# Head outputs of two attention branches with tokens on partitions: squares summed along the free axis, the mLSTM denominator as one more column, transposes back

## Chip, cores and metric

One core of a Trainium2 chip runs the whole program. The metric is the device time of one execution in microseconds (us); lower is better.

## The reference, cut to what matters

Two transformer blocks run over 256 tokens of width 1024, all in fp32. The change touches the middle of the first block, where a differential attention (8 heads of width 128) and an mLSTM (4 heads of width 256) run side by side, each head's output is RMS-normalised, and both go through a projection.

```
def diff_attention(q, k, v, lam, g_subln, lambda_init):
    ...
        a = p[:, 0] - lam * p[:, 1]
        return jnp.einsum('bhqk,bkhd->bqhd', a.astype(v.dtype), v)
    ...
    o = rmsnorm(o, g_subln) * (1.0 - lambda_init)
...
        sc = jnp.einsum('bhtd,bhsd->bhts', qc, kc) * w
        ...
        den = jnp.sum(sc, axis=-1) + w_inter * jnp.einsum('bhtd,bhd->bht', qc, n)
        h = num / jnp.maximum(jnp.abs(den), jnp.exp(-m_t))[..., None]
...
    hn = rmsnorm(hcell, g_mlnorm.reshape(H, Dh))
    y = (hn + ml_skip.reshape(H, Dh) * xch) * jax.nn.sigmoid(o_pre).reshape(B, S, H, Dh)
...
        merged = jax.nn.sigmoid(ga) * (ya @ w_proj_a[l]) + jax.nn.sigmoid(gb) * (yb @ w_proj_b[l])
```

## The kernel before

Activations lie transposed: features on the 128 partitions, the 256 tokens (T) along the free axis. A linear layer is `t_linear`: one call computes 256 output features by 16 matmuls of 128x128 weights against 256 tokens. In the trace each fp32 matmul is two records, so one call is 32 records; a transpose is one record. Weights stream through four slots of 2 MB (`W`, `slots`), fetched by SyncE in a fixed order, each as soon as its slot's last reader is done.

The order of every engine is written out by hand, one Python loop over iterations j for each engine; engines meet only at semaphores. The stretch of the change is the mixer loop of the first block, j = 0 to 31. On TensorE an iteration holds some small work of the heads and then one linear call (iterations 16 to 27: `ga`, `gb`, `op`; 28 to 31: `pa`), and after the loop come four `pb` calls. Small work around the change, by iteration:

- 12 to 19: attention scores of head j-12 (`t_da_scores`), whose softmax takes VectorE (`v_da_scores`), ScalarE (`s_da_exp`) and VectorE (`v_da_weights`) in turn. 14 to 21: transpose of the weights (`t_da_turn`, head j-14). 15 to 22: the product with the values (`t_da_mix`, head j-15), copied by ScalarE into YA (`s_da_mix`).
- 18 to 25: even, mLSTM scores (`t_ml_scores`, which also spreads two rows over all partitions as "ml b"); odd, `t_ml_mix`: the numerator, and with a block of ones the denominator, spread over all partitions.
- 24 and 26: `t_squares`, 8 matmuls that sum ScalarE's squares over the partitions, for attention ("dn") and mLSTM ("hn"). 25 to 31: `t_spread`, 12 matmuls that lay the resulting 1/rms rows over all partitions, which VectorE multiplies in (`v_da_norm`, `v_ml_out`).

PSUM banks go round in rings: `L` (banks 0 to 2: linear calls and the transposes of `t_ada_turn`), `S3` (banks 3 to 5: attention scores, two a head, attention products, mLSTM scores and numerators), `X2` (banks 6 and 7: the rest). `open` gives the next bank of a ring and waits until the user three (S3) or two (X2) places earlier has closed it. `ABT` holds attention and mLSTM weights; two of its four buffers go round as `ab`. VectorE also sums the modulation vectors from weights in the slots (`v_ada_blocks`, rows tmpA<-slots), which frees these slots.

## Time and profile before

| what | value |
|---|---|
| three runs, median (lowest, highest) | 1405.17 us (1404.03, 1406.8) |
| the profiled execution, its own time | 1407.13 us |
| its span, first to last instruction | 1405.0 us |
| TensorE busy | 1368.4 us, 97% of the span |
| VectorE, ScalarE, GpSimd busy | 586.3, 286.5, 40.6 us |
| mean granted TensorE clock | 0.995 |

The profile is of one execution; times in it are from the start of its span. L197 is the helper behind all matmuls, L200 transposes, L203 ScalarE's activations, L206, L209, L212 and L215 forms of VectorE work. A record's duration includes the pipeline's depth, and neighbours overlap, so the cost of a piece of TensorE work is read from its start to the start of the next piece. PE is TensorE, PEld its weight loads, DVE VectorE, ACT ScalarE.

### The profile page before, as it was taken

How to read it: one execution, taken by the hardware profiler on the slowest of the kernel's cores; microseconds unless marked ns; L12 is line 12 of the kernel's file. 1: busy time of each engine (PE TensorE's matmuls, PEld its weight loads, DVE VectorE, ACT ScalarE, POOL GpSimd, SP SyncE). 2: the span in 40 equal slices, each digit the busy share in tenths (PEclk: the TensorE clock that was granted, in tenths of full speed). 3: DMA queues.
4: the chain of work that ended last, by engine and by line, in shares of the span. 5: the costliest groups of instructions: out<-in, count | busy, mean ns of one | idle time of the engine just before them, and what ended most of it. 6: DMA issues, size and time to landing. Idle time of an engine off the chain costs nothing.

```text
span 1405.0 us, 17698 instructions
## 1 busy us (share of the span) xinstructions
PE 1368.4 (97%) x7428; PEld 1164.3 (83%) x7428; DVE 586.3 (42%) x1513; ACT 286.5 (20%) x770; POOL 40.6 (3%) x46
## 2 busy tenths in 40 slices
PE   4999999999999999999999999999999999899997
PEld 3888888976778877889888889988799999577777
DVE  4536440150165444544464620377643231056642
ACT  2100000221143221003000001332323321044431
POOL 0000000000110000010000000000200000000010
PEclk8999999999999999999999999999999999999999
DMA  9788854633535335585898754453300513632300
GB/s 327 231 300 288 299 176 155 229 101 114 186 110 190 108 132 180 198 298 194 298 299 288 267 181 147 156 204 121 104 17 1 180 61 120 185 91 61 121 1 30
DMA packets 170092, 236.99 MB, mean 169 GB/s; under 512 B 4924, under 2 KB 106350, under 8 KB 170014
## 3 DMA queue, kind: packets, MB, share of 16 engines
q1 hardware_dynamic: 166736, 229.40, 48.8%
q10 hardware_dynamic: 2542, 3.31, 0.7%
q0 software_dynamic: 736, 3.17, 0.6%
q8 instruction: 58, 0.95, 0.3%
q14 instruction: 20, 0.16, 0.0%
HBM read 234.79 MB, written 4.22 MB: 170 GB/s over the span
## 4 chain that ended last, share of the span: by engine, by line
PE 94%; DVE 3%; ACT 1%; DMA 1%; issue 0%; POOL 0%; SPq 0%; DVEq 0%; ACTq 0%
PE ps L197 91%; PE ps L200 4%; DMA slots<-in_w_down 1%; DMA H<-in_xT 1%; DVE tmpB L212 0%; ACT tmpC L203 0%; DVE U L212 0%; DVE tmpA L212 0%; DVE rstd L224 0%; DVE arena L212 0%; DVE mods L221 0%; ACT arena L203 0%; ACT U L203 0%; DVE arena L206 0%; POOL arena L206 0%
## 5 line engine op out<-in xcount | busy, mean ns | idle before, releaser
L197 PE MATMUL ps<-U,slots 128*128 128x256 f32 (+2 forms) x3488 | 720.1, 366 | 3.0 <-ACT U L203 2.4
L197 PEld LDWEIGHTS ps<-U,slots 128*128 128x128 f32 (+1 forms) x3488 | 618.4, 190 | 86.6 <-issue 7.5
L197 PE MATMUL ps<-arena,slots 128*128 128x256 f32 (+1 forms) x1840 | 325.8, 338 | 3.4 <-DMA slots<-in_w_down 2.6
L197 PEld LDWEIGHTS ps<-arena,slots 128*128 128x128 f32 x1840 | 292.2, 191 | 34.9 <-DMA slots<-in_w_down 3.0
L212 DVE SCALAR_TENSOR_TENSOR tmpA<-slots,sm,tmpA 128x512 f32<-128x512 f32 x182 | 139.3, 765 | 5.9
L203 ACT ACTIVATE tmpC<-ps 128x256 f32<-128x256 f32 (+3 forms) x97 | 39.8, 414 | 438.0 <-PE ps L197 426.3
L197 PE MATMUL ps<-arena 128*128 128x64 f32 (+6 forms) x736 | 110.3, 308 | 1.5 <-ACT arena L203 0.9
L197 PEld LDWEIGHTS ps<-arena 128*128 128x128 f32 (+1 forms) x736 | 90.7, 190 | 21.9 <-issue 16.1
L203 ACT ACTIVATE arena<-ps 128x512 f32<-128x512 f32 (+1 forms) x90 | 48.2, 547 | 178.2 <-PE ps L197 137.6
L212 DVE SCALAR_TENSOR_TENSOR tmpC<-tmpC,ps 128x256 f32<-128x256 f32 (+2 forms) x48 | 19.6, 407 | 140.1 <-ACT tmpC L203 140.0
L212 DVE SCALAR_TENSOR_TENSOR H<-ps,sm,H 128x256 f32<-128x256 f32 (+1 forms) x32 | 11.9, 413 | 135.4 <-PE ps L197 135.4
L203 ACT ACTIVATE tmpC<-H 128x512 f32<-128x512 f32 (+1 forms) x32 | 16.3, 520 | 240.0 <-DVE H L212 217.7
L203 ACT ACTIVATE arena<-arena,st 128x128 f32<-128x128 f32 (+2 forms) x128 | 48.4, 404 | 20.6 <-DVE st L209 20.6
L197 PE MATMUL ps<-tmpC,cst 128*128 128x128 f32 (+1 forms) x256 | 37.6, 304 | 10.9 <-ACT tmpC L203 10.8
L212 DVE SCALAR_TENSOR_TENSOR tmpB<-arena,hw,tmpB 128x256 f32<-128x256 f32 x96 | 46.5, 485 | 3.4
L197 PEld LDWEIGHTS ps<-tmpC,cst 128*128 128x128 f32 (+1 forms) x256 | 31.7, 194 | 15.1 <-issue 9.6
L212 DVE SCALAR_TENSOR_TENSOR arena<-tmpC,ps 128x512 f32<-128x512 f32 x16 | 11.0, 686 | 72.9 <-ACT tmpC L203 72.9
L203 ACT ACTIVATE U<-U,mods,sm 128x128 f32<-128x128 f32 (+1 forms) x72 | 29.9, 493 | 54.2 <-DVE sm L212 42.8
L200 PE MATMUL ps<-cst,arena 128*128 128x128 f32 (+1 forms) x288 | 39.8, 276 | 0.0
L200 PEld LDWEIGHTS ps<-cst,arena 128*128 128x128 f32 (+1 forms) x288 | 31.5, 140 | 7.5 <-issue 3.2
L227 DVE COPY arena<-ps 64x256 f32<-64x256 f32 (+4 forms) x18 | 7.8, 432 | 63.3 <-PE ps L197 63.1
L203 ACT ACT_TABLE_LOAD x24 | 30.8, 1283 | 3.9 <-issue 1.8
(142 smaller groups left out, 807.0 us busy)
## 6 DMA issues: line engine op xcount, KB each, us to landing
slots<-in_w_ada SPq DMA_DIRECT2D x14, 2048.0 KB, 7.9
slots<-in_w_in SPq DMA_DIRECT2D x14, 2048.0 KB, 8.0
slots<-in_ada_w SPq DMA_DIRECT2D x12, 2048.0 KB, 8.1
slots<-in_w_down SPq DMA_DIRECT2D x16, 1408.0 KB, 6.9
slots<-in_w_gate SPq DMA_DIRECT2D x19, 1024.0 KB, 5.6
slots<-in_w_up SPq DMA_DIRECT2D x19, 1024.0 KB, 8.6
slots<-in_a_in_w SPq DMA_DIRECT2D x8, 2048.0 KB, 8.9
slots<-in_b_in_w SPq DMA_DIRECT2D x12, 1024.0 KB, 5.6
```

Source lines behind the costliest of these rows:

```text
L197: return Nothing() if self.e is None else self.e.matmul(*a, **k)
L200: return Nothing() if self.e is None else self.e.transpose(*a, **k)
L203: return Nothing() if self.e is None else self.e.activation(*a, **k)
L212: return Nothing() if self.e is None else self.e.scalar_tensor_tensor(out=o, in0=i0, scalar=s, in1=i1, op0=op0, op1=op1)
L227: return Nothing() if self.e is None else self.e.tensor_copy(*a)
```

## The change

Both products are computed the other way round: the attention weights or mLSTM scores are the stationary operand and the values move, so that an output has tokens on partitions and a head's features along the free axis.

- `t_da_mix` is three matmuls of 128 columns instead of one of 256 and one of 128. ScalarE sums squares along the free axis as it reads the bank (`accum_out`), and VectorE and ScalarE make the 1/rms of all 16 (head, token half) columns in three small steps. VectorE scales YA (`v_da_scale`, iterations 24 and 25), TensorE transposes it back (`t_da_flip`, 26 and 27, two calls of four transposes each), and ScalarE copies with the gain (`s_da_norm`).
- `t_ml_mix` is three matmuls of 257 columns: MV has a column of ones behind each head, so that column 256 is the denominator. It takes two banks of S3, one for each token half, and waits for both at its start. The matmuls with a block of ones are gone. ScalarE reads each bank four times (`s_ml_mix`). The division is folded into the normalisation, and `v_hn_scale` (26 and 27), `t_hn_flip` (28 to 31, four transposes each) and `v_ml_out` follow.
- "ml b" spreads one row instead of two; the floor row becomes a column by two more small transposes in `t_ml_source` (iteration 13), which now also wait for ScalarE's exponential of that row.
- `t_squares`, `t_spread` and their partners are gone, and the constant `selc` with them (64 columns). The skip term is scaled by ScalarE beforehand (`s_skip`, one in each iteration from 18 to 25). One memset writes the ones.

Not shown in the diff: `v_da_mean`, `s_da_root`, `v_da_rstd`, `v_hn_mean`, `s_hn_root` and `v_hn_rstd` work on at most 16 columns; `v_hn_scale` and `t_hn_flip` are to mLSTM what `v_da_scale` and `t_da_flip` are to attention, one call a head. Lines of which only the removal matters are left to the listing above.

```diff
-        def t_squares(e, n, row_of, to=X):
...
-            for h in range(8):
-                e.wait_ge(*act.at(n, "sq", h // 2))
-                e.matmul(ps[0:8, 0:T], selc[:, row_of(h), :], TC.buf(n, "sq", h // 2)[:, h % 2 * T:h % 2 * T + T], start=h == 0,
-                         stop=h == 7).then_inc(*pe.up(n, "sq", h))
-        def t_spread(e, n, h, row, to=X):
...
-            e.matmul(ps[:, 0:T], row_to_all(h, 8), row).then_inc(*pe.up(n, "row", h))
...
         def t_da_mix(e, h):
...
-            aT = at_.buf("da", h)
-            e.matmul(ps[:, 0:T], VA[:, 0, h * P:(h + 1) * P], aT[:, 0:T], start=True, stop=False)
-            e.matmul(ps[:, 128:T], VA[:, 1, h * P:(h + 1) * P], aT[:, 256:384], start=False, stop=True).then_inc(*pe.up("da mix", h))
+            aT, v0, v1 = at_.buf("da", h), VA[:, 0, h * P:(h + 1) * P], VA[:, 1, h * P:(h + 1) * P]
+            e.matmul(ps[:, 0:P], aT[:, 0:P], v0)
+            e.matmul(ps[:, P:T], aT[:, P:T], v0, start=True, stop=False)
+            e.matmul(ps[:, P:T], aT[:, T:384], v1, start=False, stop=True).then_inc(*pe.up("da mix", h))
             at_.close([pe.now()], "da", h)
         def s_da_mix(e, h):
+            ps = S3.buf("da mix", h)
             e.wait_ge(*pe.at("da mix", h))
-            e.activation(YA[:, h, :], S3.buf("da mix", h)[:, 0:T], ACT.Copy).then_inc(*act.up("ya", h))
+            e.activation(YA[:, h, :], ps[:, 0:T], ACT.Copy).then_inc(*act.up("ya", h))
+            for i in range(2):
...
+                e.activation(jk, ps[:, i * P:(i + 1) * P], ACT.Square, accum_out=ss[:, 2 * h + i:2 * h + i + 1]).then_inc(*act.up())
+                JK.close([act.now()], "da", h, i)
+            act.mark("ya sq", h)
             S3.close([act.now()], "da mix", h)
...
+        def v_da_scale(e, g):
+            y = YA[:, 2 * g:2 * g + 2, :].rearrange("p h (i n) -> p (h i) n", i=2)
+            e.wait_ge(*dve.at("dn rstd"))
+            e.wait_ge(*act.at("ya", 2 * g + 1))
+            e.tensor_tensor(y, y, ss[:, 4 * g:4 * g + 4].unsqueeze(2).to_broadcast([P, 4, P]), ALU.mult).then_inc(*dve.up("dn", g))
+        def t_da_flip(e, g):
...
+            e.wait_ge(*dve.at("dn", g))
+            for n in range(4):
+                i = e.transpose(ps[:, n * P:(n + 1) * P], YA[:, 2 * g + n // 2, n % 2 * P:n % 2 * P + P], ident)
+            i.then_inc(*pe.up("da flip", g))
+        def s_da_norm(e, g):
+            e.wait_ge(*pe.at("da flip", g))
+            e.activation(YA[:, 2 * g:2 * g + 2, :], two(X2.buf("da flip", g)), ACT.Copy, scale=V("g_subln")).then_inc(*act.up("ya out", g))
+            X2.close([act.now()], "da flip", g)
...
-        MV = arena[:, 14368:16416].rearrange("p (i n) -> p i n", i=2)
+        MV = arena[:, 14368:16424].rearrange("p (i h n) -> p i h n", i=2, h=4)
...
-            e.matmul(ps, row_to_all(h, 4), R[0:4, 4:6, :]).then_inc(*pe.up("ml b", h))
+            e.matmul(ps[:, 0:T], row_to_all(h, 4), R[0:4, 4, :]).then_inc(*pe.up("ml b", h))
...
         def t_ml_mix(e, h):
             sc = ab.buf("ml", h)
-            np_, free = S3.open("ml n", h)
-            for f in free:
+            n0, free = S3.open("ml n", h, 0)
+            n1, free2 = S3.open("ml n", h, 1)
+            for f in free + free2:
                 e.wait_ge(*f)
             e.wait_ge(*dve.at("ml sc", h))
-            for e2 in range(2):
-                o = h * T + e2 * P
-                e.matmul(np_[:, e2 * T:(e2 + 1) * T], MV[:, 0, o:o + P], sc[:, 0:T], start=True, stop=False)
-                i = e.matmul(np_[:, e2 * T + P:(e2 + 1) * T], MV[:, 1, o:o + P], sc[:, T:384], start=False, stop=True)
-            i.then_inc(*pe.up("ml n", h))
-            dp, free = X2.open("ml den", h)
-            for f in free:
-                e.wait_ge(*f)
-            e.matmul(dp[:, 0:T], C("ones"), sc[:, 0:T], start=True, stop=False)
-            e.matmul(dp[:, P:T], C("ones"), sc[:, T:384], start=False, stop=True).then_inc(*pe.up("ml den", h))
+            e.wait_ge(*dve.at("ml ones"))
+            e.matmul(n0[:, 0:257], sc[:, 0:P], MV[:, 0, h, :])
+            e.matmul(n1[:, 0:257], sc[:, P:T], MV[:, 0, h, :], start=True, stop=False)
+            e.matmul(n1[:, 0:257], sc[:, T:384], MV[:, 1, h, :], start=False, stop=True).then_inc(*pe.up("ml n", h))
             ab.close([pe.now()], "ml", h)
...
+        HT = HC.rearrange("p (h i) n -> p h i n", i=2)
+        den, hsq = gates[:, :, 24:28], gates[:, :, 20:24]
+        hs2 = gates[:, :, 28:36].rearrange("p i (n h) -> p i n h", n=2)
+        def s_ml_mix(e, h):
             e.wait_ge(*pe.at("ml n", h))
+            for i in range(2):
+                ps = S3.buf("ml n", h, i)
+                e.activation(HT[:, h, i, :], ps[:, 0:T], ACT.Copy).then_inc(*act.up("ht", h, i))
+                e.activation(den[:, i, h:h + 1], ps[:, T:257], ACT.Abs).then_inc(*act.up())
+                for n in range(2):
...
+                    e.activation(jk, ps[:, n * P:(n + 1) * P], ACT.Square, accum_out=hs2[:, i, n, h:h + 1]).then_inc(*act.up())
+                    JK.close([act.now()], "ml", h, i, n)
+                S3.close([act.now()], "ml n", h, i)
+            act.mark("ht sq", h)
...
+        def s_skip(e, c):
+            e.wait_ge(*pe.at("mk", 3))
+            e.activation(XC[:, c, :], XC[:, c, :], ACT.Copy, scale=sm[:, 120 + c:121 + c]).then_inc(*act.up("skip", c))
...
                     t_ml_source(e)
                 if 18 <= j < 26:
                     (t_ml_mix if j % 2 else t_ml_scores)(e, (j - 18) // 2)
-                if j == 24:
-                    t_squares(e, "dn", lambda h: h, X2)
-                if 25 <= j < 29:
-                    t_spread(e, "dn", 2 * j - 50, r8, X2)
-                    t_spread(e, "dn", 2 * j - 49, r8, X2)
-                if j == 26:
-                    t_squares(e, "hn", lambda c: c // 2, X2)
+                if 26 <= j < 28:
+                    t_da_flip(e, 2 * j - 52)
+                    t_da_flip(e, 2 * j - 51)
                 if 28 <= j < 32:
-                    t_spread(e, "hn", j - 28, r8h, X2)
+                    t_hn_flip(e, j - 28)
                 if j >= 18 and j % 4 == 2:
                     t_ada_turn(e, 12 + (j - 18) // 4)
                 if j < 4:
...
                 elif j < 28:
                     t_linear(e, ("ga", "gb", "op")[(j - 16) // 4], j % 4, U, u_in("n2"))
                 else:
-                    t_linear(e, "pa", j - 28, YA, lambda k, half: dve.at("ya", k))
+                    t_linear(e, "pa", j - 28, YA, lambda k, half: act.at("ya out", k // 2))
...
                     v_da_scores(e, j - 12)
                 if 10 <= j < 18:
                     v_rotate(e, ("q", "k")[j % 2], (j - 10) // 2)
-                if 18 <= j < 26:
-                    (v_ml_mix if j % 2 else v_ml_scores)(e, (j - 18) // 2)
+                if 18 <= j < 26 and j % 2 == 0:
+                    v_ml_scores(e, (j - 18) // 2)
                 if j == 24:
-                    v_mean(e, "dn", 1.0 / 128, 0.8, r8, X2)
-                    v_rstd(e, "dn", r8)
-                if 25 <= j < 29:
-                    v_da_norm(e, 2 * j - 50)
-                    v_da_norm(e, 2 * j - 49)
+                    v_da_mean(e)
+                    v_da_rstd(e)
+                if 24 <= j < 26:
+                    v_da_scale(e, 2 * j - 48)
+                    v_da_scale(e, 2 * j - 47)
                 if j == 26:
-                    v_mean(e, "hn", 1.0 / 256, 1.0, r8h, X2)
-                    v_rstd(e, "hn", r8h)
+                    v_hn_mean(e)
+                    v_hn_rstd(e)
+                if 26 <= j < 28:
+                    v_hn_scale(e, 2 * j - 52)
+                    v_hn_scale(e, 2 * j - 51)
                 if 28 <= j < 32:
                     v_ml_out(e, j - 28)
                 if j >= 29:
...
                 if j == 13:
                     s_ml_floor(e)
                 if 18 <= j < 26:
-                    (s_ml_den if j % 2 else s_ml_weights)(e, (j - 18) // 2)
+                    (s_ml_mix if j % 2 else s_ml_weights)(e, (j - 18) // 2)
+                    s_skip(e, j - 18)
                 if 12 <= j < 20:
                     s_da_exp(e, j - 12)
-                if j == 23:
-                    s_squares(e, "dn", YA, lambda h: act.at("ya", h))
                 if j == 24:
-                    s_rstd(e, "dn", r8)
-                if j == 25:
-                    s_squares(e, "hn", HC, lambda c: dve.at("hc", c))
+                    s_da_root(e)
                 if j == 26:
-                    s_rstd(e, "hn", r8h)
+                    s_hn_root(e)
+                if 26 <= j < 28:
+                    s_da_norm(e, 2 * j - 52)
+                    s_da_norm(e, 2 * j - 51)
```

In iteration 19 TensorE has, before, the transposes of attention head 5 (into ps6), the scores of head 7 (ps5 and ps3, q and k from arena), and the numerator (ps4) and denominator (ps7) of mLSTM head 0; the buffer numbers are the banks:

```order
L200 MATMUL ps6<-cst,ABT 128x128 x3
L197 MATMUL ps5<-arena 128x128
L197 MATMUL ps5<-arena 128x256
L197 MATMUL ps3<-arena 128x128
L197 MATMUL ps3<-arena 128x256
L197 MATMUL ps4<-ABT,arena 128x256
L197 MATMUL ps4<-ABT,arena 128x128
L197 MATMUL ps4<-ABT,arena 128x256
L197 MATMUL ps4<-ABT,arena 128x128
L197 MATMUL ps7<-ABT,cst 128x256
L197 MATMUL ps7<-ABT,cst 128x128
L197 MATMUL ps1<-U,slots 128x256 x16
```

and with the change:

```order
L196 MATMUL ps6<-cst,ABT 128x128 x3
L193 MATMUL ps5<-arena 128x128
L193 MATMUL ps5<-arena 128x256
L193 MATMUL ps3<-arena 128x128
L193 MATMUL ps3<-arena 128x256
L193 MATMUL ps4<-arena,ABT 128x257
L193 MATMUL ps5<-arena,ABT 128x257 x2
L193 MATMUL ps1<-U,slots 128x256 x16
```

Six matmuls, all with 256 or 128 columns, have become three of 257 columns, and their second bank is ps5, which the first scores of head 7 were written to just ahead.

In iterations 26 to 29 TensorE has, before, spreads (ps<-rows,cst), the sums of mLSTM squares (ps<-tmpC,cst), a modulation transpose (ps<-cst,tmpA) and the linear calls:

```order
L197 MATMUL ps<-rows,cst 128x256 x2
L197 MATMUL ps<-tmpC,cst 8x256 x8
L200 MATMUL ps<-cst,tmpA 128x128 x4
L197 MATMUL ps<-U,slots 128x256 x16
L197 MATMUL ps<-rows,cst 128x256 x2
L197 MATMUL ps<-U,slots 128x256 x16
L197 MATMUL ps<-rows,cst 128x256 x3
L197 MATMUL ps<-arena,slots 128x256 x16
L197 MATMUL ps<-rows,cst 128x256
L197 MATMUL ps<-arena,slots 128x256 x16
```

and with the change:

```order
L196 MATMUL ps<-cst,arena 128x128 x8
L196 MATMUL ps<-cst,tmpA 128x128 x4
L193 MATMUL ps<-U,slots 128x256 x16
L196 MATMUL ps<-cst,arena 128x128 x8
L193 MATMUL ps<-U,slots 128x256 x16
L196 MATMUL ps<-cst,arena 128x128 x4
L193 MATMUL ps<-arena,slots 128x256 x16
L196 MATMUL ps<-cst,arena 128x128 x4
L193 MATMUL ps<-arena,slots 128x256 x16
```

Each spread, and the sums of squares, have made way for transposes of YA and HC (ps<-cst,arena); the linear calls stand as they did.

## Rows read from the trace of the kernel before

**Rows 1.** The page: busy times (first section), and shares of the chain that ended last.

```profile
PE 1368.4 (97%) x7428; PEld 1164.3 (83%) x7428; DVE 586.3 (42%) x1513; ACT 286.5 (20%) x770; POOL 40.6 (3%) x46
...
PE 94%; DVE 3%; ACT 1%; DMA 1%; issue 0%; POOL 0%; SPq 0%; DVEq 0%; ACTq 0%
```

**Rows 2.** Windows: stretch, length, busy of PE, PEld, DVE, ACT, POOL, clock, DMA.

```profile
445.00:583.50 138.50, 138.22 (x656) 111.24 (x656) 64.54 (x136) 31.05 (x68) 0.00 (x0) 1.00 0.46 164
```

**Rows 3.** Timeline of PE, iterations 18 and 19: start, length, operation, records.

```profile
446.55 1.12 PE L197 MATMUL ps<-rows,cst 4*128 4x512 f32 x2
447.60 1.57 PE L197 MATMUL ps<-arena 128*128 128x256 f32 x8
...
456.36 0.82 PE L197 MATMUL ps<-ABT,arena 128*128 128x256 f32 x4
457.01 0.49 PE L200 MATMUL ps<-cst,ABT 128*128 128x128 f32 x3
...
458.30 1.57 PE L197 MATMUL ps<-ABT,arena 128*128 128x256 f32 x8
...
460.36 7.07 PE L197 MATMUL ps<-U,slots 128*128 128x256 f32 x32
```

**Rows 4.** Timeline of PE, iterations 24 and 25.

```profile
509.64 3.62 PE L197 MATMUL ps<-tmpC,cst 128*8 128x256 f32 x16
513.20 7.17 PE L197 MATMUL ps<-U,slots 128*128 128x256 f32 x32
...
522.26 1.24 PE L197 MATMUL ps<-rows,cst 8*128 8x256 f32 x4
523.43 7.17 PE L197 MATMUL ps<-U,slots 128*128 128x256 f32 x32
```

**Rows 5.** Timeline of PE, iterations 28 to 31 and three calls behind them.

```profile
552.90 7.17 PE L197 MATMUL ps<-arena,slots 128*128 128x256 f32 x32
560.00 0.69 PE L197 MATMUL ps<-rows,cst 8*128 8x256 f32 x2
560.62 7.17 PE L197 MATMUL ps<-arena,slots 128*128 128x256 f32 x32
...
576.47 27.89 PE L197 MATMUL ps<-arena,slots 128*128 128x256 f32 x128
```

**Rows 6.** Timeline of PE, eight full transposes in iteration 9.

```profile
353.23 1.04 PE L200 MATMUL ps<-cst,arena 128*128 128x128 f32 x8
354.10 7.15 PE L197 MATMUL ps<-U,slots 128*128 128x256 f32 x32
```

**Rows 7.** Groups of PE by form: records, busy us, mean ns of one.

```profile
L197 PE MATMUL ps<-arena,slots 128*128 128x128 f32 x736 | 84.5, 275 | 0.0
```

**Rows 8.** Timeline of VectorE, iteration 19: weights of head 6, then scores of head 7.

```profile
457.61 0.29 DVE L209 TENSOR_SCALAR ABT<-arena,st 128x128 f32<-128x128 f32 x1 [4.96 <-PE ps L200]
...
459.20 0.42 DVE L215 CUSTOM_DVE_ANT_0 arena<-ps,cst 128x256 f32<-128x256 f32 x1
...
459.54 0.29 DVE L215 CUSTOM_DVE_ANT_0 arena<-ps,cst 128x128 f32<-128x128 f32 x1
```

**Rows 9.** Timeline of ScalarE, iteration 19: exponentials with accumulated sums.

```profile
460.84 0.39 ACT L203 ACTIVATE arena<-arena,st 128x128 f32<-128x128 f32 x1
...
461.23 0.50 ACT L203 ACTIVATE arena<-arena,st 128x256 f32<-128x256 f32 x1
```

**Rows 10.** Groups of ScalarE by form, 399 to 585 us.

```profile
L203 ACT ACTIVATE arena<-ps 128x256 f32<-128x256 f32 x8 | 3.1, 383 | 0.3
```

**Rows 11.** DMA: issue in SyncE's timeline.

```profile
565.71 0.37 SPq L233 DMA_DIRECT2D slots<-in_w_proj_b  x1
```

**Rows 12.** DMA issues of the page: KB each, us from issue to landing.

```profile
slots<-in_w_proj_b SPq DMA_DIRECT2D x2, 2048.0 KB, 9.7
```

**Rows 13.** Windows, columns as in rows 2: behind an idle stretch, and among transposes.

```profile
20.00:28.00 8.00, 1.48 (x5) 1.11 (x6) 7.04 (x12) 1.09 (x2) 0.00 (x0) 0.65 1.10 348
1027.00:1049.00 22.00, 21.75 (x200) 21.64 (x200) 10.63 (x25) 4.18 (x7) 0.00 (x0) 1.00 0.01 1
```

More of the change, by code:

```diff
@@ L325, in build @@
         one_row = rows[0:8, 7, :]
-        r8, r8h = rows[0:8, 0, :], rows[0:8, 3, :]
         def parts(key):
@@ L1040, in build @@
         TILES = [(0, 0, 128, 128), (1, 128, 384, 0)]
+        JK = ring(*[arena[:, 21416 + P * n:21544 + P * n] for n in range(3)])
+        ss = sm[:, 140:156]
         def t_da_scores(e, h):
@@ new lines, in t_da_flip @@
+        def t_da_flip(e, g):
+            ps, free = X2.open("da flip", g)
+            for f in free:
+                e.wait_ge(*f)
+            e.wait_ge(*dve.at("dn", g))
[6 more added lines that the diff above has]
+            X2.close([act.now()], "da flip", g)
@@ L1339, in s_ml_weights @@
         def s_ml_weights(e, h):
[L1340 to L1343 removed]
+            w_ = TB.buf("ml", h)
             e.wait_ge(*dve.at("ml d", h))
[L1345 removed]
             e.wait_ge(*dve.at("ml source"))
@@ L1371, in t_ml_mix, with v_hn_rstd, v_hn_scale, t_hn_flip @@
+        def v_hn_rstd(e):
+            e.wait_ge(*act.at("hn root"))
+            e.reciprocal(hsq, hsq).then_inc(*dve.up("hn rstd"))
+        def v_hn_scale(e, h):
+            e.wait_ge(*dve.at("hn rstd"))
+            e.tensor_tensor(HT[:, h, :, :], HT[:, h, :, :], hsq[:, :, h:h + 1].to_broadcast([P, 2, T]), ALU.mult).then_inc(*dve.up("hn", h))
+        def t_hn_flip(e, h):
+            ps, free = X2.open("hn flip", h)
             for f in free:
                 e.wait_ge(*f)
-            e.wait_ge(*dve.at("ml sc", h))
@@ L1404, in v_ml_out @@
-        def v_ml_out(e, h):
-            ps = X2.buf("hn", "row", h)
-            e.wait_ge(*pe.at("hn", "row", h))
+            e.wait_ge(*dve.at("hn", h))
+            for n in range(4):
+                j = e.transpose(ps[:, n * P:(n + 1) * P], HT[:, h, n % 2, n // 2 * P:n // 2 * P + P], ident)
+            j.then_inc(*pe.up("hn flip", h))
+        def s_skip(e, c):
+            e.wait_ge(*pe.at("mk", 3))
+            e.activation(XC[:, c, :], XC[:, c, :], ACT.Copy, scale=sm[:, 120 + c:121 + c]).then_inc(*act.up("skip", c))
@@ L2489, in vector @@
             e.memset(XM[:, :, 0:3], 0.0).then_inc(*dve.up("xm pads"))
+            e.memset(MV[:, :, :, T:257], 1.0).then_inc(*dve.up("ml ones"))
             e.wait_ge(*dve.at("xm pads"))
```

124 lines of the change are left out of this document (50 added, 74 removed).

## The prediction

> **What bounds the kernel now.** I read the page first. TensorE is busy for 97% of the span and has 94% of the chain that ended last; the other engines are at 42% or less [rows 1]. A change is therefore worth what it does to TensorE's own list of work, plus any wait that it puts into that list. The windows view says the same of the stretch that is changed: from 445.0 to 583.5 us TensorE is busy for 138.22 of 138.50 us at a clock of 1.00, VectorE for 64.5 and ScalarE for 31.1 us [rows 2]. So there is almost no wait to win here. I then priced each piece by the timeline of TensorE, from its start to the next piece's start, since the printed durations overlap.
>
> **What TensorE loses.**
> - "ml b" with two rows (512 columns) takes 1.05 us, 446.55 to 447.60 [rows 3]. One row of 256 columns over all partitions is what a single spread is, 0.62 us, 560.00 to 560.62 [rows 5]. Four times 0.43: −1.7 us.
> - Numerator and denominator of an mLSTM head take 2.06 us, 458.30 to 460.36 [rows 3], of 1152 columns in all. In their place stand three matmuls of 257 columns. No row has that width; four calls in a row give 27.89 us for 64 matmuls of 256 columns, 0.436 us each [rows 5], so three take about 1.31 us (one column more is under 1%). The edges to neighbouring work cost some 0.05 us that stay: 0.70 us less, four times, −2.8 us. The lower end is nothing more than this, the upper end for an odd width that streams badly is the price of the old piece: 0 instead of −2.8.
> - The sums of squares go: 8 matmuls in 3.56 us, 509.64 to 513.20 [rows 4], twice: −7.1 us.
> - The spreads go: two in 1.17 us, 522.26 to 523.43 [rows 4], one alone in 0.62 [rows 5]; twelve at 0.60 are −7.2 us.
> - A linear call in front of a spread takes 7.10 us, 552.90 to 560.00, against 6.97 (27.89 / 4) without one [rows 5]. Six such edges: −0.8 us.
>
> **What TensorE gains.**
> - 32 full transposes of YA and HC and two tiny ones. Eight transposes take 0.87 us, 353.23 to 354.10 [rows 6], 0.109 us each: 34 × 0.109 = +3.7 us. Their upper bound is the price of an ordinary matmul of 128 columns, 0.23 us (below), which would be +7.8; I take 0.109 because the row is of the same operation from the same memory.
> - The attention product becomes three matmuls of 128 columns. Before it takes 0.65 us, 456.36 to 457.01 [rows 3]. Of 128-column records 736 take 84.5 us, 0.115 each, two a matmul [rows 7]: 0.23 us, so three are 0.69. The changed operand roles cost no extra loads that show: +0.04, eight times, +0.3 us.
>
> **Waits that the change adds.** A numerator now takes two banks of S3 where it took one, and waits for both at its start. In iteration 19 its second bank (ps5) holds the first scores of attention head 7, which TensorE wrote just ahead. VectorE frees that bank only after the weights of head 6, which themselves wait for the transposes of head 5 on TensorE. Before, VectorE starts these weights at 457.61, begins the last reduction of the first scores at 459.20 and goes over to the second bank at 459.54 [rows 8]; with its accumulator read the bank is free at about 459.6, and a semaphore later, 459.7, TensorE may go on. TensorE was at the numerator at 458.30 [rows 3]. Both sides hang on the same transposes, so the distance stays: **+1.4 us**, once. Behind the waiting matmul stand linear call 19 and all later work. In iterations 21, 23 and 25 there are no new attention scores, and the places three earlier in the ring are banks that ScalarE emptied, or VectorE read for the scores that the numerator needs in any case; I cost them at nothing.
>
> ScalarE gets more to do. An accumulating activation of 128 columns takes 0.39 us to the next start, 460.84 to 461.23 [rows 9], a copy of 256 columns 0.38 [rows 10]. `s_da_mix` grows by 0.8 us, `s_ml_mix` is at most 8 × 0.39 = 3.1 us, `s_skip` 0.4. The fullest iteration, 19, has 18 activations, about 18 × 0.4 = 7 us, against more than 8 on TensorE (a linear call of 7.0 and a numerator of 1.3 alone); readers need its results an iteration later. In iterations 20 to 25 the exponentials are gone. VectorE gets less to do. For nothing I also take the memset, the additional wait in `t_ml_source` (the exponential behind it is short and ScalarE has the time), and the smaller constant; if any shows, it is a few tenths.
>
> The transposes back wait for long chains, but with an iteration of about 7 us between each link and its reader: squares of head 7 in iteration 22, roots and scaling in 24 and 25, `t_da_flip` from 26; numerator of head 3 in 25, root and scaling in 26 and 27, `t_hn_flip` from 28. Its bank in X2 was emptied by ScalarE an iteration before. That is the cover; a link that took more than 7 us would lose it, and each microsecond over would be lost once.
>
> **Weights.** A faster TensorE asks for weights sooner. The first `pb` block is issued at 565.71 [rows 11] and lands 9.7 us later [rows 12], at 575.4; its call starts one linear call behind 576.47, at 583.4 [rows 5]. That leaves 8 us. The issue hangs on VectorE's sum in iteration 29, which follows TensorE, so issue and reader move together; work of only about 1 us is removed between them. Behind the stretch nothing is changed, and each fetch is released by a reader, so the gain should be carried to the end.
>
> **Sum.** −1.7 − 2.8 − 7.1 − 7.2 − 0.8 + 3.7 + 0.3 + 1.4 = −14.2 us. The profiled execution took 1407.13 us, so one like it would take 1392.9. The median of the three runs is 2.0 us lower, 1405.17; from it I get **1391.0 us**.
>
> **Rivals.**
> 1. *The wait in iteration 19 is not alone.* The ring of three banks is short for a numerator of two. If ScalarE's four reads a bank are slower from PSUM than the rows say, mLSTM scores and attention products in iterations 20 to 24 wait for banks too. At 1.4 us, as in iteration 19, for each of three more iterations it would be −14.2 + 4.2, about 1395.2 us. Or the odd width costs its 2.8 us, about 1393.8. For it: such waits come from ScalarE's order, which is fixed. Against it: ScalarE is busy for only 31.1 of 138.5 us [rows 2].
> 2. *No wait at all.* If something ahead on TensorE takes the 1.4 us, 1389.6 us. Rows 8 speak against it.
> 3. *The gain is given back to the weights.* If transfers, and not readers, set the pace behind 583 us, up to all 14.2 us are lost: 1403 to 1405 us, no change. Against it are the 8 us above.
> 4. *Slower: the clock falls.* At 20 to 28 us TensorE has idle stretches and its granted clock is 0.65 [rows 13]. If the wait in iteration 19 and then groups of up to 12 transposes did the same, the 60 us of work from 523.43 [rows 4] to 583.4 would run at 1.2 instead of 2.4 GHz: +60 − 14.2, about 1451 us. It decides for slower as soon as more than 14 us of work run at the lower level. Against it: from 1027 to 1049 us TensorE alternates transposes with short matmuls, and the clock is 1.00 [rows 13]. The Trainium skill has this rule ("TensorE: Matmul & The Clock Gate", Part 4: PE-mode transpose): transposes don't count as busy TensorE for the clock gate. By that rule the change puts 32 of them where full matmuls stood; the trace has not borne it out where other matmuls stand between them.
> 5. *The change is not what it says,* as where another instruction holds what was removed. The built order shows that it is there, so this has next to nothing.
>
> **How the numbers follow.** The forecast (1388 to 1394) has 0.77, rival 1 has 0.13, rival 2 0.03 (within the same range), rival 3 0.03, rival 4 and other mishaps over 14 us 0.04. A measurement of this kernel tells about 0.2%, 2.8 us, from no change. Faster: 0.77 + 0.13 + 0.03 = 0.93; same 0.03; slower 0.04. The range goes from no wait with a low run (runs lie 1.1 us under their median) and edges a little better, 1387, to rival 1 with a high run (1.6 us over), 1397.
>
> **What would show it.** Right: TensorE's list from the start of iteration 18 to the first `pb` call about 14 us shorter; no matmul of sums or spreads; about 1.3 us for a numerator; 0.44 us for four transposes; one wait of 1.4 us in iteration 19, put down to VectorE; the clock at 1.00. Wrong: idle time of TensorE behind ScalarE in iterations 20 to 25, or behind VectorE or ScalarE at a transpose in 26 to 31; waits for weights behind 570 us; numerators near 2 us.

## The result, and the profile after

The changed kernel takes 1389.7 us, the median of 4 runs (1388.76 to 1390.4), beside 1404.6 us for the kernel before (4 runs, 1403.61 to 1406.8). The ratio is 0.9889, with an interval of 0.9877 to 0.9901: 14.9 us less. The forecast was 1391.0, with a range of 1387 to 1397. The profiled execution took 1389.24 us, with a span of 1387.1.

The page of the changed kernel, busy times and shares of the chain that ended last, answers to [rows 1]:

```profile
PE 1351.4 (97%) x7398; PEld 1158.6 (84%) x7398; DVE 569.2 (41%) x1493; ACT 295.7 (21%) x846; POOL 40.7 (3%) x46
...
PE 94%; DVE 3%; ACT 1%; DMA 1%; issue 0%; POOL 0%; SPq 0%; DVEq 0%; ACTq 0%
```

TensorE is busy for 17.0 us less and is still the bound, with the same 97% of the span and 94% of the chain. VectorE lost 17.1 us, and ScalarE has 9.2 us more in 76 more instructions; the experiments below ask whether either shows in the time. (In the kernel after, L193 is the matmul, L196 the transpose, L199 ScalarE's activation, L202 to L211 VectorE and L229 the DMA of SyncE.)

**How the two traces are compared.** Spans differ by 17.9 us, medians by 14.9, so a span is the wrong measure. I take the *stretch* instead: from the start of the first "ml b" in iteration 18 to the start of the last `pa` call in iteration 31. It holds every part of TensorE's change but the two tiny transposes of `t_ml_source` and the first four of the eight attention products (iterations 15 to 18). These are TensorE's rows at its two ends in the kernel after (start, length, operation, records):

```profile
445.34 0.69 PE L193 MATMUL ps<-rows,cst 4*128 4x256 f32 x2
445.96 1.57 PE L193 MATMUL ps<-arena 128*128 128x256 f32 x8
...
560.17 15.06 PE L193 MATMUL ps<-arena,slots 128*128 128x256 f32 x69
```

445.34 to 560.17 is 114.83 us. Before, it is 446.55 [rows 3] to 576.47 [rows 5], 129.92 us. The stretch is **15.09 us** shorter. The rest of the spans' difference is 1.21 us ahead of 445 and 1.60 us behind 560; the second traces below show that the change doesn't gain these. What the change does ahead of the stretch costs 0.19 us (0.13 the two transposes, 0.06 the four products): from the start of TensorE's first small work in iteration 13 to the stretch are 49.74 us (395.60 to 445.34), where 49.55 stood (397.00 to 446.55).

The windows view of the kernel after, same columns as [rows 2], over the stretch and over the part of it in which 32 full transposes stand:

```profile
445.30:560.20 114.90, 113.49 (x572) 98.93 (x571) 43.94 (x107) 37.39 (x126) 0.00 (x0) 1.00 0.53 187
...
521.20:560.20 39.00, 39.00 (x203) 34.56 (x201) 17.28 (x35) 8.36 (x12) 0.00 (x0) 1.00 0.57 202
```

TensorE idles for 1.41 us (114.90 − 113.49), all of it in iteration 19. Behind that it works without a gap. ScalarE does 37.39 us of work where it did 31.05 in a longer window, and TensorE doesn't feel it.

TensorE's timeline of the kernel after in iterations 19 and 21. A bracket holds the idle time ahead of an operation and its releaser, the work whose end let it start:

```profile
458.15 1.54 PE L193 MATMUL ps<-arena,ABT 128*128 128x257 f32 x6 [1.41 <-DVE st L211]
459.52 7.07 PE L193 MATMUL ps<-U,slots 128*128 128x256 f32 x32
...
477.45 1.47 PE L193 MATMUL ps<-arena,ABT 128*128 128x257 f32 x6
478.76 7.07 PE L193 MATMUL ps<-U,slots 128*128 128x256 f32 x32
```

TensorE's work on the scores of head 7 ends at 456.74 (458.15 − 1.41); then it stands until 458.15. A numerator takes 1.37 us (458.15 to 459.52), where numerator and denominator took 2.06 [rows 3], and in iteration 21 1.31 us with no wait (477.45 to 478.76), where they took 1.96. The releaser is VectorE's accumulator read. Here is VectorE in the same iteration of the kernel after, as in [rows 8]:

```profile
455.99 0.29 DVE L205 TENSOR_SCALAR ABT<-arena,st 128x128 f32<-128x128 f32 x1 [4.87 <-PE ps L196]
...
457.92 0.08 DVE L211 DVE_READ_ACCUMULATOR2_ANT st<- 128x1 f32 x1
```

VectorE sits idle for 4.87 us until TensorE's transposes come, does the weights of head 6 and then the first scores of head 7, and frees their bank at 458.00; 0.15 us later TensorE starts.

The transposes back, in TensorE's timeline of the kernel after, iterations 26 to 31:

```profile
521.26 1.04 PE L196 MATMUL ps<-cst,arena 128*128 128x128 f32 x8
522.13 0.60 PE L196 MATMUL ps<-cst,tmpA 128*128 128x128 f32 x4
...
537.26 0.60 PE L196 MATMUL ps<-cst,arena 128*128 128x128 f32 x4
537.70 7.07 PE L193 MATMUL ps<-arena,slots 128*128 128x256 f32 x32
544.60 0.60 PE L196 MATMUL ps<-cst,arena 128*128 128x128 f32 x4
```

Eight take 0.87 us (521.26 to 522.13) and four 0.44 (537.26 to 537.70). None has a bracket: no link of the long chains that the transposes wait for came late. The linear call ahead of a group of four, 537.70 to 544.60, takes 6.90 us; the same call ahead of a spread took 7.10, 552.90 to 560.00 [rows 5].

### The profile page after: what moved, and what is told of

It is laid out like the page before. It is cut to its first block, busy times and chain, and to the rows that moved or that the text cites. A ratio compares the mean times of both kernels' runs of the same rounds, so it can differ in the third digit from the quotient of the medians.

```text
span 1387.1 us, 17688 instructions
## 1 busy us (share of the span) xinstructions
PE 1351.4 (97%) x7398; PEld 1158.6 (84%) x7398; DVE 569.2 (41%) x1493; ACT 295.7 (21%) x846; POOL 40.7 (3%) x46
## 4 chain that ended last, share of the span: by engine, by line
PE 94%; DVE 3%; ACT 1%; DMA 1%; issue 0%; POOL 0%; SPq 0%; DVEq 0%; ACTq 0%
PE ps L193 91%; PE ps L196 4%; DMA H<-in_xT 1%; DVE tmpB L208 0%; DMA slots<-in_w_down 0%; ACT tmpC L199 0%; DVE U L208 0%; DVE tmpA L208 0%; DVE rstd L220 0%; DVE mods L217 0%; ACT arena L199 0%; ACT U L199 0%; DVE arena L208 0%; DVE arena L202 0%; POOL arena L202 0%
## 5 line engine op out<-in xcount | busy, mean ns | idle before, releaser
L193 PE MATMUL ps<-U,slots 128*128 128x256 f32 (+2 forms) x3488 | 719.5, 366 | 3.0 <-ACT U L199 2.4
L193 PEld LDWEIGHTS ps<-U,slots 128*128 128x128 f32 (+1 forms) x3488 | 618.5, 190 | 85.6 <-issue 6.7
L193 PE MATMUL ps<-arena,slots 128*128 128x256 f32 (+1 forms) x1840 | 325.5, 338 | 1.9 <-DMA slots<-in_w_down 1.2
L193 PEld LDWEIGHTS ps<-arena,slots 128*128 128x128 f32 x1840 | 292.2, 191 | 32.5 <-DMA slots<-in_w_down 1.6
L199 ACT ACTIVATE tmpC<-ps 128x256 f32<-128x256 f32 (+3 forms) x89 | 36.7, 416 | 426.3 <-PE ps L193 419.7
L193 PE MATMUL ps<-arena 128*128 128x64 f32 (+6 forms) x736 | 110.3, 308 | 1.5 <-ACT arena L199 0.9
L193 PEld LDWEIGHTS ps<-arena 128*128 128x128 f32 (+1 forms) x736 | 90.7, 190 | 20.2 <-issue 13.5
L199 ACT ACTIVATE arena<-ps 128x512 f32<-128x512 f32 (+2 forms) x130 | 58.5, 474 | 183.9 <-PE ps L193 143.3
L199 ACT ACTIVATE tmpC<-H 128x512 f32<-128x512 f32 (+1 forms) x32 | 16.3, 520 | 235.8 <-DVE H L208 213.5
L199 ACT ACTIVATE arena<-arena,st 128x128 f32<-128x128 f32 (+2 forms) x128 | 48.5, 405 | 19.2 <-DVE st L205 19.2
L196 PE MATMUL ps<-cst,arena 128*128 128x128 f32 x320 | 44.3, 276 | 0.0
L196 PEld LDWEIGHTS ps<-cst,arena 128*128 128x128 f32 x320 | 35.4, 140 | 8.1 <-issue 3.2
L199 ACT ACTIVATE U<-U,mods,sm 128x128 f32<-128x128 f32 (+1 forms) x72 | 29.9, 493 | 53.9 <-DVE sm L208 42.4
L193 PE MATMUL ps<-tmpC,cst 128*128 128x128 f32 x224 | 29.7, 290 | 10.3 <-ACT tmpC L199 10.3
L193 PEld LDWEIGHTS ps<-tmpC,cst 128*128 128x128 f32 x224 | 28.4, 205 | 10.5 <-issue 9.2
```

Of the source, the lines that this page charges most:

```text
L193: return Nothing() if self.e is None else self.e.matmul(*a, **k)
L196: return Nothing() if self.e is None else self.e.transpose(*a, **k)
L199: return Nothing() if self.e is None else self.e.activation(*a, **k)
```

## The experiments

The theory is that of the prediction: TensorE's list sets the time, each part is worth its rows, and one wait of 1.4 us is the price of a numerator in two banks, the second of which VectorE frees late in its own order. Four things were open: whether the parts add up; whether the wait is VectorE's order (and could be had back) or the ring itself; whether ScalarE's added work costs something; and which part of the 17.9 us by the spans belongs to the execution rather than to the change.

**One half alone.** The first kernel is the kernel before with the attention part (products with tokens on partitions, sums on ScalarE, `t_da_flip`). The second is the kernel after with the attention part as before.

```diff
 attention half alone, against before
-            e.matmul(ps[:, 0:T], VA[:, 0, h * P:(h + 1) * P], aT[:, 0:T], start=True, stop=False)
...
+            e.matmul(ps[:, 0:P], aT[:, 0:P], v0)
...
-                if j == 24:
-                    t_squares(e, "dn", lambda h: h, X2)
...
+                if 26 <= j < 28:
+                    t_da_flip(e, 2 * j - 52)
...
```

> The kernel before with the attention half of the change alone (product the other way round, squares along the free axis, transposes back); the mLSTM half is as before, only that its sums of squares use a bank of ring L, since two banks of X2 are taken by the transposes. Theory (TensorE's own list and one wait of the mLSTM half): minus 3.6 us of sums, minus 4.8 us of eight spreads, minus 0.4 us of edges, plus 1.7 us of 16 transposes, products unchanged: about -7 us (0.995), and no wait in iteration 19. Rival (the attention half is free elsewhere or pays with waits of its own at the transposes): nearer to 0.

Measured: 1398.54 us against 1405.05, ratio 0.9952 (0.994 to 0.9964), 6.5 us less. Its timeline of TensorE, the ends of the stretch and the old numerator of iteration 19:

```profile
446.33 1.12 PE L197 MATMUL ps<-rows,cst 4*128 4x512 f32 x2
...
458.09 1.57 PE L197 MATMUL ps<-ABT,arena 128*128 128x256 f32 x8
...
569.16 11.06 PE L197 MATMUL ps<-arena,slots 128*128 128x256 f32 x50
```

The stretch is 122.83 us, 7.09 less than before. The numerator (458.09), which takes one bank here, has no bracket: it doesn't wait.

```diff
 mLSTM half alone, against after
-                if 26 <= j < 28:
-                    t_da_flip(e, 2 * j - 52)
-                    t_da_flip(e, 2 * j - 51)
+                if j == 24:
+                    t_squares(e, "dn", lambda h: h, X2)
+                if 25 <= j < 29:
+                    t_spread(e, "dn", 2 * j - 50, r8, X2)
+                    t_spread(e, "dn", 2 * j - 49, r8, X2)
```

> The changed kernel with the attention half as before and the mLSTM half changed. Theory: minus 1.7 (one row instead of two), minus 2.8 (numerators with a column of ones), minus 3.6 (sums), minus 2.5 (four spreads), minus 0.4 (edges), plus 1.8 (16 transposes), plus 1.4 (the wait in iteration 19, which is this half's): about -8 us (0.994), with the wait in the trace. Together with attn_only it gives the whole. Rival: the halves don't add up, because one needs the other's room in the banks.

Measured: 1397.37 us against 1405.05, ratio 0.9944 (0.9932 to 0.9957), 7.7 us less. The same places in its timeline of TensorE:

```profile
446.32 0.69 PE L197 MATMUL ps<-rows,cst 4*128 4x256 f32 x2
...
459.12 1.54 PE L197 MATMUL ps<-arena,ABT 128*128 128x257 f32 x6 [1.41 <-DVE st L215]
...
568.21 12.04 PE L197 MATMUL ps<-arena,slots 128*128 128x256 f32 x55
```

The stretch is 121.89 us, 8.03 less, with the whole wait of 1.41 in it. The halves give −7.09 − 8.03 = −15.12 us, the whole −15.09. The parts add up, and the wait belongs to the mLSTM half alone. Whether it is that half's second bank, and VectorE's order, the next two edits ask.

**The wait taken away by order.** VectorE does the scores of head 7 ahead of the weights of head 6, in iteration 19 alone, and the numerator waits for its second bank only behind its first matmul.

```diff
 against after
-            for f in free + free2:
+            for f in free:
...
             e.matmul(n0[:, 0:257], sc[:, 0:P], MV[:, 0, h, :])
+            for f in free2:
+                e.wait_ge(*f)
...
+                if j == 19:
+                    v_da_scores(e, 7)
...
-                if 12 <= j < 20:
+                if 12 <= j < 19:
```

> The changed kernel with the wait of iteration 19 taken away: VectorE reduces the scores of head 7 before it makes the weights of head 6 (in that iteration alone), and TensorE waits for the numerator's second bank only behind the first of its three matmuls. Theory: the wait of 1.41 us goes, nothing else is late, -1.4 us against the changed kernel, some -16 us against before. Rival: the weights of head 6 or ScalarE's exponentials become late and give it back: 0 against the changed kernel.

Measured: 1388.31 us against 1405.05, ratio 0.9879 (0.9866 to 0.9893). Its timeline of TensorE, and one row of TensorE's weight loads:

```profile
444.66 0.69 PE L193 MATMUL ps<-rows,cst 4*128 4x256 f32 x2
...
455.99 1.93 PE L193 MATMUL ps<-arena,ABT 128*128 128x257 f32 x6
457.75 1.46 PE L193 MATMUL ps<-U,slots 128*128 128x256 f32 x6
...
558.40 21.96 PE L193 MATMUL ps<-arena,slots 128*128 128x256 f32 x101
```

```profile
456.78 0.73 PEld L193 LDWEIGHTS ps<-arena,ABT 128*128 128x128 f32 x4 [0.50 <-DVE st L211]
```

The stretch is 113.74 us, 1.09 less than after. The wait ahead of the numerator is gone, but the numerator takes 1.76 us (455.99 to 457.75) instead of 1.37: 0.39 us are left between its first and second matmul, where the weight load waits for VectorE. So the wait hung on VectorE's order, and three quarters of it can be had back.

The edit does two things at once, and neither was run alone. An estimate parts them: VectorE is done with the scores in the second bank at 456.72, and by 0.15 us of hand-over and 1.37 us for a numerator that waits for both banks at its start, linear call 19 would begin at 458.24. In the kernel after it begins 14.18 us into the stretch (459.52 − 445.34), here that would be 458.84, and it does begin at 457.75. So some 0.6 us are VectorE's order and 0.5 the later wait.

**The wait lengthened.** VectorE's `v_ada_blocks` of iteration 19, two modulation sums that stand at its end, are put ahead of the scores. If the numerator waits for these scores, the whole length of the sums must show in the time.

```diff
 against after
+                if j == 19:
+                    v_ada_blocks(e, 12, 10, 12)
                 if 12 <= j < 20:
                     v_da_scores(e, j - 12)
...
-                if j >= 14:
+                if j >= 14 and j != 19:
```

> The changed kernel; in iteration 19 VectorE's two modulation sums (1.5 us) stand between the weights of head 6 and the scores of head 7 instead of behind the scores. Theory: TensorE's wait ahead of the numerator of head 0 grows by their length, from 1.4 to 2.9 us, and the time by 1.5 us against the changed kernel. Rival (the numerator waits for its first bank, which ScalarE reads, or for its weights): no change.

Measured: 1391.58 us against 1404.2, ratio 0.9908 (0.9894 to 0.9923). TensorE's timeline:

```profile
446.44 0.69 PE L193 MATMUL ps<-rows,cst 4*128 4x256 f32 x2
...
460.70 0.67 PE L193 MATMUL ps<-arena,ABT 128*128 128x257 f32 x2 [2.85 <-DVE st L211]
...
562.72 17.65 PE L193 MATMUL ps<-arena,slots 128*128 128x256 f32 x81
```

The wait grows from 1.41 to 2.85 us and the stretch from 114.83 to 116.28: 1.44 and 1.45. A microsecond of VectorE at this one place is a microsecond of the kernel, although VectorE is busy for about 41% only.

**Transposes as matmuls.** The same data against the identity, in the same places, as ordinary fp32 matmuls.

```diff
 against after, in t_da_flip (t_hn_flip has the same edit)
-                i = e.transpose(ps[:, n * P:(n + 1) * P], YA[:, 2 * g + n // 2, n % 2 * P:n % 2 * P + P], ident)
+                i = e.matmul(ps[:, n * P:(n + 1) * P], YA[:, 2 * g + n // 2, n % 2 * P:n % 2 * P + P], ident)
```

> The changed kernel with the 32 transposes back done as ordinary matmuls with the identity as moving operand. The prediction had 0.109 us for a transpose and 0.23 us for a matmul of 128 columns as its upper bound. Theory: 32 x 0.12 = +3.8 us against the changed kernel, eight of them in 1.8 us instead of 0.87. Rival (both are bound by loading the same 128 stationary columns): no change.

Measured: 1393.26 us against 1404.2, ratio 0.9921 (0.9906 to 0.9936). TensorE's timeline at the first eight and at the ends, then the window over all 32:

```profile
521.17 1.95 PE L193 MATMUL ps<-cst,arena 128*128 128x128 f32 x16
522.96 0.60 PE L196 MATMUL ps<-cst,tmpA 128*128 128x128 f32 x4
...
445.25 0.69 PE L193 MATMUL ps<-rows,cst 4*128 4x256 f32 x2
...
563.72 16.57 PE L193 MATMUL ps<-arena,slots 128*128 128x256 f32 x76
...
521.00:564.00 43.00, 43.00 (x236) 38.82 (x235) 17.34 (x36) 8.58 (x12) 0.00 (x0) 1.00 0.54 193
```

Eight take 1.79 us (521.17 to 522.96) instead of 0.87, and the stretch is 118.47 us, 3.64 more. The rows agree: as matmuls the transposes cost 32 × 0.224 = 7.2 instead of 3.5 us. The prediction had this form as the upper bound of its term. The clock is 1.00 in both forms.

**More work for ScalarE.** Two more copies of 256 columns, each behind a wait for the one before, in front of every later step of a bank of the numerator: 16 copies, which also free the banks later.

```diff
 against after, in s_ml_mix
-                e.activation(HT[:, h, i, :], ps[:, 0:T], ACT.Copy).then_inc(*act.up("ht", h, i))
+                e.activation(HT[:, h, i, :], ps[:, 0:T], ACT.Copy).then_inc(*act.up())
+                for _ in range(2):
+                    e.wait_ge(*act.now())
+                    e.activation(HT[:, h, i, :], ps[:, 0:T], ACT.Copy).then_inc(*act.up())
+                act.mark("ht", h, i)
```

> The changed kernel; ScalarE copies each numerator bank three times instead of once, which adds 16 copies of about 0.4 us with their waits to iterations 19, 21, 23 and 25, 6 to 8 us in all. Theory: ScalarE has the time, no change (within 0.3 us). Rival (ScalarE's hold on the banks of S3 is near its limit): waits of TensorE for ScalarE at the mLSTM scores of iterations 20, 22 and 24, +1 us or more.

Measured: 1389.31 us against 1404.2, ratio 0.989 (0.9873 to 0.9906). TensorE's ends of the stretch, and ScalarE's timeline in iteration 19:

```profile
446.24 0.69 PE L193 MATMUL ps<-rows,cst 4*128 4x256 f32 x2
...
561.07 19.16 PE L193 MATMUL ps<-arena,slots 128*128 128x256 f32 x88
```

```profile
460.62 1.21 ACT L199 ACTIVATE arena<-ps 128x256 f32<-128x256 f32 x3 [2.85 <-PE ps L193]
461.73 0.17 ACT L199 ACTIVATE gates<-ps 128x1 f32<-128x1 f32 x1
```

The three copies take 1.11 us (460.62 to 461.73), and the stretch is 114.83 us, the same as after to the hundredth. ScalarE's added work costs nothing, and it still costs nothing with 16 more copies.

**Both kernels again, unchanged.**

> The changed kernel itself, for comparison on the same chip. Theory: about -15 us against before; TensorE's list from the spread of iteration 18 to the pa call of iteration 31 shorter by 15.0 us as in the first profile, whereas the 1.4 us ahead of the mixer loop and the 1.6 us behind the stretch, by which that profile was shorter too, belong to the profiled executions and not to the change, so they should look otherwise here. Rival: the smaller constant (start) and the weights of the second feed-forward network (tail) gain these 3 us in each execution.

> The kernel before itself, for a second profile of it. Theory: start of iteration 13 and the wait for weights in the second feed-forward network differ between its two profiles by about as much as they do between before and after. Rival: they stand where they stood, and the changed kernel really gains there.

Measured: after 1390.17 us against 1405.05, ratio 0.9888 (0.9873 to 0.9903); before, one run, 1404.51 us, span 1402.4. TensorE's timeline of the second trace of after, then of the second trace of before, and last the row behind the stretch from the first trace of before:

```profile
446.71 0.69 PE L193 MATMUL ps<-rows,cst 4*128 4x256 f32 x2
...
561.54 18.73 PE L193 MATMUL ps<-arena,slots 128*128 128x256 f32 x86
```

```profile
445.57 1.12 PE L197 MATMUL ps<-rows,cst 4*128 4x512 f32 x2
...
575.49 4.80 PE L197 MATMUL ps<-arena,slots 128*128 128x256 f32 x21
...
826.04 4.15 PE L197 MATMUL ps<-arena,slots 128*128 128x256 f32 x18 [1.03 <-DMA slots<-in_w_down]
```

```profile
828.65 3.72 PE L197 MATMUL ps<-arena,slots 128*128 128x256 f32 x16 [2.65 <-DMA slots<-in_w_down]
```

The stretch repeats exactly: 114.83 us (446.71 to 561.54) and 129.92 (445.57 to 575.49). What lies around it does not. The stretch starts at 445.34 and 446.71 in the two traces of after, at 446.55 and 445.57 in those of before: which kernel starts it earlier is chance (over all twelve traces it starts between 444.66 and 446.71). The wait for the `w_down` weights behind it is 2.65 us in the first trace of before and 1.03 in the second, where the kernel is the same. The second trace of before against the first of after: −0.23 ahead of the stretch, −15.09 in it, +0.02 behind it (826.91 and 826.93 us). Of all twelve traces eleven have 826.7 to 827.2 us behind the stretch; only the first of before has 828.5. The 17.9 us by the spans were 14.9 us of change (15.09 less the 0.19 ahead of the stretch) and 3.0 us of executions.

**The scores first on TensorE too.** If VectorE gets its scores early, TensorE might not have to wait for the bank at all.

```diff
 against after
             for j in range(32):
+                if j == 19:
+                    t_da_scores(e, 7)
...
-                if 12 <= j < 20:
+                if 12 <= j < 19:
...
 (VectorE's order as in the kernel above, without the split of the waits)
```

> The changed kernel; in iteration 19 both TensorE and VectorE take the scores of head 7 first: on TensorE ahead of the attention product and the transposes of head 5, on VectorE ahead of the weights of head 6. The numerator keeps its wait for both banks at the start. In swap_split 0.39 us of the wait were left, between the first and the second matmul of the numerator. Theory: the product and transposes (1.0 us) on TensorE now cover VectorE's two reductions (1.2 us from the first scores on), so no idle time is left in iteration 19 and the stretch from the spread of iteration 18 to the last pa call is 1.41 us shorter than in the changed kernel (113.4 instead of 114.83 us); time about -1.4 us against the changed kernel. Rival: the wait moves to the attention product or to the transposes, and up to 0.4 us stay.

> As swap_split, for comparison on the same chip: stretch 113.74 us, 0.3 us longer than scores_first, which the times can't tell apart.

Measured: 1387.87 us against 1403.92, ratio 0.988 (0.9863 to 0.9896); beside it, the kernel with VectorE's swap and the split wait once more, 1388.5, ratio 0.9886 (0.9871 to 0.9901). TensorE's timeline of the first:

```profile
446.36 0.69 PE L193 MATMUL ps<-rows,cst 4*128 4x256 f32 x2
...
458.13 1.54 PE L193 MATMUL ps<-arena,ABT 128*128 128x257 f32 x6 [0.18 <-DVE st L211]
...
560.16 20.02 PE L193 MATMUL ps<-arena,slots 128*128 128x256 f32 x92
```

The stretch is 113.80 us, where 113.4 was expected. This expectation was missed: I had the whole wait gone. With the scores at the head of the iteration, the numerator's second bank is, in the ring of three, that of the second scores instead of the first, and VectorE frees it at 457.98, 0.15 us before TensorE starts; 0.18 us of wait stay. The rest of the 0.38 us that are missing lies in neighbours: the linear call ahead of the scores takes 7.00 us where it took 6.91, the product behind them 0.77 where it took 0.67. The stretches of the two versions differ by 0.06 us (113.80, and 113.74 twice), which their times can't show. Both are 1.0 to 1.1 us shorter than the kernel after in each trace; where the swap ran beside the kernel after, on one chip, its median was 1.86 us lower (1388.31 and 1390.17), though the intervals overlap. They are the best versions I ran, 15 to 17 us below before.

## Why the prediction was right, point by point

- **What bounds it.** TensorE's list did set the time. The stretch lost 15.09 us, the change in all 14.90 (15.09 less the 0.19 ahead of the stretch), and the median 14.9.
- **"ml b".** Two rows of 512 columns were to lose 0.43 us each time; 445.34 to 445.96 is 0.62, where 1.05 stood: −1.72 against −1.7.
- **Numerators.** 1.37, 1.31, 1.30 and 1.30 us, 5.28 in all against 8.04: −2.76 against −2.8. The odd width of 257 costs nothing that can be read, and that part of rival 1 has fallen.
- **Sums of squares and spreads.** They are gone: −7.11 against −7.1, and −7.25 against −7.2.
- **Transposes.** 0.87 us for eight and 0.44 for four: +3.5 in the stretch and +0.13 in `t_ml_source` (0.21 us before, 398.82 to 399.03; 0.34 now, 397.41 to 397.75), against +3.7. Taking the price of the row of the same operation instead of the matmul's was right; the matmul's price, forced by the edit above, adds 3.64 us.
- **Products.** 0.66 to 0.67 us against 0.65: +0.1 for all eight, half of it in the stretch, where +0.3 stood. The price of 0.115 us a record was a group's busy time shared out; start to start, three products in a row are at 0.22 us each, 0.11 a record.
- **The wait.** 1.41 us, once, in iteration 19, by VectorE, as forecast. The halves show that it is the mLSTM half's, the swap with the later wait that it hangs on the second bank and VectorE's order, the delay that it goes into the time one for one. Rival 2 has fallen. Iterations 20 to 25 have no wait, so rival 1 has fallen too. The wait added in `t_ml_source` doesn't show either: its row has no bracket.
- **Edges.** This term was mis-sized, and it was a small one. What is left of the stretch is −15.09 + 13.87 = −1.22 us, where −0.8 stood. The 6.97 us for a call without a spread came from a printed duration (27.89 / 4), which the prediction itself had ruled out as a price. From start to start the four calls take 27.73 us before (576.47 to 604.20) and 27.63 after (560.17 to 587.80), 6.91 each in the latter. These are the rows behind the four calls in TensorE's timeline, first of the kernel before, then of the kernel after:

```profile
604.20 0.60 PE L200 MATMUL ps<-cst,tmpA 128*128 128x128 f32 x4
```

```profile
587.80 0.60 PE L196 MATMUL ps<-cst,tmpA 128*128 128x128 f32 x4
```

  In TensorE's timeline of before, a linear call takes 6.91 us between neighbours of 128 rows and 128 columns of weights, 7.00 to 7.01 with a spread, a sum of squares or other weights of few rows or columns on one side, and 7.10 to 7.11 with them on both. After the change the calls of iterations 24 to 30 all take 6.90 to 6.91: −1.08 us with 0.01 of iteration 21. The rest is at the mLSTM scores of iteration 24 and two modulation transposes, which also lost such neighbours (−0.2), and at the work ahead of the wait (+0.06). Why a neighbour costs this, no run shows.
- **ScalarE and VectorE at nothing.** Right, with much room. `s_ml_mix` took 1.64 us (459.72 to 461.36) and not the 3.1 that I took for an upper bound, as the rows of the last section show.
- **Weights.** The forecast had a margin of 8 us for the first `pb` block. SyncE's row of its issue, and the page's DMA row (KB each, us from issue to landing), in the kernel after:

```profile
549.18 0.37 SPq L229 DMA_DIRECT2D slots<-in_w_proj_b  x1
...
slots<-in_w_proj_b SPq DMA_DIRECT2D x2, 2048.0 KB, 9.0
```

  It lands at about 558.2 and is wanted at 567.1 (one call of 6.91 behind 560.17): 8.9 us. Issue and reader moved together, 16.5 and 16.3 us. Rival 3 has fallen.
- **The clock.** The granted clock is 1.00, the level of 2.4 GHz, over the 39 us with the 32 transposes and over the whole stretch with its wait, and with the wait lengthened by 1.44 us the stretch grew by 1.45, so that no loss of clock came with it. Rival 4 has fallen: its 60 us loss isn't there. The Trainium skill ("TensorE: Matmul & The Clock Gate", Part 4: PE-mode transpose) says that transposes don't count as busy TensorE in the same way for the clock gate. The trace doesn't contradict that for a program of transposes alone, which none here is; in groups of up to twelve between linear calls of 7 us the granted clock stays at 1.00.

The change in all gained 14.90 us, and the sum was 14.2: 0.4 of the difference is in the edges, 0.2 in the products and 0.07 in the transposes. All three err to the same side, so nothing here came right by cancelling. Of the 1.3 us between the forecast of 1391.0 and the 1389.7 measured, 0.7 are these, and 0.6 the median of before (1405.17 then, 1404.6 with a fourth run). The step from the profiled execution to the median held too: of the 2.6 us between the two profiled executions of before, 1.62 are the `w_down` wait (2.65 and 1.03 us) and 0.98 the start (446.55 and 445.57).

## What to carry to other kernels

In a kernel that one engine bounds, price each edit by that engine's own list, start to start, from the row that is nearest in operation and width; seven terms came out within 0.5 us each, the two worst being those taken from a printed duration and from a group's busy time. A lightly used engine mattered at only one place. Where a step takes two buffers of a ring in which it took one, look up who holds the second and what stands ahead of its release on that engine; here that cost 1.4 us, of which a swap of two steps on VectorE and a later wait on TensorE together gave back 1.1. To compare two traces, choose a stretch that holds as much of the change and as little else as can be, and look at what lies ahead of it: it repeated to 0.01 us, while spans of one kernel differed by 2.6 us.

## What the runs showed of the hardware

ScalarE's work on the first bank of a numerator, and the first row behind its second bank, in its timeline of the kernel after:

```profile
459.72 0.38 ACT L199 ACTIVATE arena<-ps 128x256 f32<-128x256 f32 x1 [2.86 <-PE ps L193]
460.00 0.17 ACT L199 ACTIVATE gates<-ps 128x1 f32<-128x1 f32 x1
460.05 0.28 ACT L199 ACTIVATE arena<-ps 128x128 f32<-128x128 f32 x1
460.21 0.21 ACT L199 ACTIVATION_READ_ACCUMULATOR arena<-ps 128x1 f32 x1
460.30 0.29 ACT L199 ACTIVATE arena<-ps 128x128 f32<-128x128 f32 x1
...
461.36 0.56 ACT L199 ACTIVATE arena<-arena,sm 128x256 f32<-128x256 f32 x1
```

- A one-column activation from PSUM behind another costs 0.05 us to the next start (460.00 to 460.05), although its own length is 0.17. A square of 128 columns with its sum costs 0.25 us (460.05 to 460.30): 0.16 and an accumulator read of 0.09. I had priced it from an exponential with its sum, 0.39 [rows 9], which reads `arena` and not a bank, and takes its bias from `st`. The Trainium skill ("ScalarE: Activation LUTs", What ACT_TABLE_LOAD costs) gives about 93 ns more for each operand of one column that an activation reads; the difference here is 0.14 us, in that direction, and no run separates the bias from what is read and from the function.
- A transpose of 128x128 fp32 costs 0.109 us in a row of eight, an ordinary matmul on the same data 0.224 (1.79 us for eight): a factor of about 2.1.
- A matmul of 257 fp32 columns costs 0.43 to 0.44 us (1.30 to 1.31 for three), as one of 256 (27.63 for 64).
- From the end of VectorE's read (458.00) to TensorE's start behind the semaphore (458.15) pass 0.15 us. It is the same with the scores first (457.98 to 458.13) and with the wait lengthened (460.55 to 460.70).
- A linear call of 16 matmuls takes 6.91 us between neighbours of full size and about 0.1 us more for each side on which TensorE works with weights of 4, 8 or 64 rows, or of 8 columns (7.00 and 7.10).
